# Two column groups of the modulation and the first token block's end, moved into the second feed-forward

## The chip, the cores and the metric

The kernel runs on one core of a Trainium2 chip, in float32. The metric is the device time of one execution in microseconds, in the median of several runs.

## The reference

A transformer block with an mLSTM and one with latent attention, each followed by a PEER layer (top-16 experts out of 16384 for each of 8 heads, gathered by index) and a gated projection, and behind them one modulated block. 256 tokens of width 1024. What the change touches lies in the modulated block:

```python
mod = jax.nn.silu(c) @ w_ada[l] + b_ada[l]
sh1, sc1, g1, sh2, sc2, g2 = jnp.split(mod[:, None, :], 6, axis=-1)
h = modulate(rmsnorm(x, norm_mix_g[l]), sh1, sc1)
x = x + g1 * hybrid_mixer(h, ...)
h = modulate(rmsnorm(x, norm_ffn_g[l]), sh2, sc2)
x = x + g2 * swiglu(h, w_ffn_gate[l], w_ffn_up[l], w_ffn_down[l])
...
return rmsnorm(x, norm_final_g)
```

`w_ada` is 1024 x 6144. `g2`, the last of the six, is its last 1024 columns; it is first used behind the down projection of the feed-forward.

## The kernel before, in words

The 256 tokens are two token blocks (`tb` 0 and 1) of 128. Every engine has its own program, written out by hand; semaphores tie them together. The dense work is cut into slots (generators that all engines step through in the same order). Four windows of expert gathering (two layers by two token blocks) run first, and slots of the token block whose experts are done are woven between the groups of the gathering. All of the modulated block for token block 0, its down projection excepted, is woven into the fourth window. Behind that window stand, with no gathering beside them: the end of the PEER layer and the gated projection for token block 1 (`sum_slots(1, 1)`, `ple_slots(1, 1)`), the mixer for token block 1 (`hybrid_slots(1)`), the mixer's output projection (`out_piece`), the second half of token block 0's down projection (`dnB`), the feed-forward of token block 1 (`ffn_slots(1)`) and its down projection (`dn`).

Weights go through a ring of NW = 4 slots of 128 x 4096 floats. `take` on TensorE records a load in program order and waits for it; SyncE issues the recorded loads in this order, one queue, and load number i first waits until the last reader of load i - 4 is done (L1276). `last_use` or `done` records that reader. `aux` puts other transfers in the same queue. A tile of 1024 x 512 weights is 2048 KB.

The modulation's matrix is used in column groups of 512. Group j through the ring: `ada_load(j)` on TensorE records the load; `ada_part(j)` on VectorE waits for the load and forms the weighted sum over its 8 row chunks in place (one tensor_scalar, L1882, and seven scalar_tensor_tensor, L1884); `ada_sum(j)` on TensorE waits for that and multiplies the sum with a matrix of ones, and it is the last reader of the slot; `ada_gate(j)` on VectorE (L1906) adds the result to the bias in `N["g2"]`. Groups 10 and 11 are `g2`. Before, their four steps stand in `hybrid_slots(1)`: load at the end of slot s, part in s + 2, sum at the start of s + 3, gate in s + 4, with s = 5 for group 10 and s = 9 for group 11.

Slots of `hybrid_slots(1)` around them on TensorE: cmp projection in 2 and 3, `nq` in 4 and 5, `kk` in 6 and 7, the compression matmuls (`compress`, two loads of 1 MB, k and v) in 7, first scores and the compression's gather matmuls (`gather_compressed`) in 9, `vv` (280 columns, 1120 KB) in 10, the second layer of the compression in 11, `bq` in 12 and 13, `bk` in 14 and 15, `bv` in 16 and 17, then four merge gates, two merge projections.

`ffn_slots(tb)` on TensorE: for each of six groups of up to 512 hidden columns (FGROUPS; the sixth has 256) a gate tile `fg` and an up tile `fu`, each one load and 64 matmuls of 128 x 128 (32 in the sixth). ScalarE evacuates `fg` with Silu, VectorE multiplies with `fu` (`product`, L2541). Down group g waits for product g.

The first token block's end on VectorE: behind the two additions of `dnB` (L2592) the multiplication with `g2` (L2594), `gated_add(0)` (L2505) and `final_norm(0)` (sum of squares L2322, a square root on ScalarE, L2583), then the copy to `out` by SyncE behind all loads.

Of the kernel before, what the change touches and what calls it, by code (L numbers as in the profile page):

```python
# [10 lines left out]
ALU = mybir.AluOpType  # L11
# [48 lines left out]
ADA_GATES = (10, 11)  # L60
# [38 lines left out]
NSA_BEFORE = (0, 2 * len(NSA_HEADS[0]))  # L99
SB_BEFORE = (0, len(SB_HEADS[0]))  # L100

ADA_AT = {5: 10, 9: 11}

PLAN = ((FIRST_SLOTS, 5, GROUPS - 4), (NEXT_SLOTS, 0, GROUPS - 2), (NEXT_SLOTS, 0, GROUPS - 2), (LAST_SLOTS, 0, GROUPS - 2))

# [48 lines left out]
def program(nc, a, out, ctx, dbg):  # L154
# [186 lines left out]
    def _(pe):  # L341
# [36 lines left out]
        def last_use(rec, name):  # L378
            b, k = place[name]
            rec["done"] = (bank_full[b], k + 1)  # L380

        def ada_load(j):
            i = nw[0]
            nw[0] += 1
            rec = dict(kind="w", src=rows(a["w_ada_2"][0], j * 512, 512), slot=i % NW, i=i, kc=KC, n=512, p=P, done=None)
            loads.append(rec)
            ada_order.append(j)
            ada_at[j] = (i % NW, 16 * (i // NW + 1), rec)

        def ada_sum(j):  # L390
            slot, _, rec = ada_at[j]
            pe.wait_ge(sem("ada_part"), ada_order.index(j) + 1)
            o = open_(f"ada{j}")
            close(mm(o[:, :], ones[:, :], ring[:, slot, (KC - 1) * 512:KC * 512]), f"ada{j}")
            last_use(rec, f"ada{j}")
# [495 lines left out]
        def ffn_slots(tb):  # L891
            await_T("xT7", tb)
            for g, chs in enumerate(FGROUPS):
                n = len(chs) * P
                for nm, w_dram in ((f"fg{tb}_{g}", a["w_ffn_gate_2"][0]), (f"fu{tb}_{g}", a["w_ffn_up_2"][0])):
                    w, rec = take(rows(w_dram, chs[0] * P, n), KC, n)
                    o = open_(nm)
                    for e in range(len(chs)):
                        ins = feat(o, e * P, w, xT, slice(e * P, (e + 1) * P), range(KC), KC, cols(tb))
                        if e % 2 == 1:  # L900
                            if e == len(chs) - 1:
                                close(ins, nm)
                                last_use(rec, nm)
                            yield f"ffn {nm} {e}"
            yield "ffn last silu"
            yield "ffn last product"
# [33 lines left out]
        def hybrid_slots(tb):  # L940
# [201 lines left out]
                    close(mm(o[:, 0:16], maskQ[:, kv * P:(kv + 1) * P], gatherT[:, :]), nm)  # L1142

            for i in range(plan["n"]):
                if tb == 1:
                    for s, j in ADA_AT.items():
                        if i == s + 3:
                            ada_sum(j)
                for g, s in enumerate(plan["nsa"]):
                    if i == s + 4:  # L1150
                        nT(g)
# [62 lines left out]
                for half in range(2):  # L1214
# [3 lines left out]
                    if i == plan["yb"] + half:  # L1218
                        moved(pe, f"bO_{tb}")
                        merge("yb", a["w_proj_b_2"][0], X["obT"], half)  # L1220
                if tb == 1 and i in ADA_AT:
                    ada_load(ADA_AT[i])
                yield f"hybrid {i}"

        def last_slots():
# [181 lines left out]
    def _(act):  # L1407
# [16 lines left out]
        def sqrt(n):  # L1424
            nsq[0] += 1
            act.wait_ge(sem("var_ready"), nsq[0])
            f(sdv[:, 0:n], var[:, 0:n], ACT.Sqrt).then_inc(sem("sd_ready"), 1)
# [361 lines left out]
        def ffn_slots(tb):  # L1789
            for g, chs in enumerate(FGROUPS):  # L1790
                for x in range(2):
                    for e in range(-(-len(chs) // 2)):
                        if x == 1 and e == 0:
                            evac(f"fg{tb}_{g}", B[tb]["hid"][:, chs[0]:chs[-1] + 1, :], split(len(chs)), fn=ACT.Silu)
                        yield f"ffn {g} {x} {e}"
            yield "ffn last silu"
            yield "ffn last product"
# [18 lines left out]
            pass  # L1816
        sqrt(1)
        evac_norm("xT7", 1, 1)
        sqrt(1)
        for _ in ffn_slots(1):  # L1820
            pass
        sqrt(1)

    @block.vector
    def _(dve):
# [52 lines left out]
        def ada_part(j):  # L1878
            slot, loaded, _ = ada_at[j]
            dve.wait_ge(slot_loaded[slot], loaded)  # L1880
            w = ring[:, slot, :].rearrange("p (k n) -> p k n", k=KC)
            step(v.tensor_scalar(w[:, 0, :], w[:, 0, :], scT[:, 0:1], None, ALU.mult))  # L1882
            for k in range(1, KC):
                ins = v.scalar_tensor_tensor(w[:, k, :], w[:, k, :], scT[:, k:k + 1], w[:, k - 1, :], ALU.mult, ALU.add)  # L1884
                if k < KC - 1:
                    step(ins)
            ins.then_inc(sem("ada_part"), 1)
# [456 lines left out]
        def hybrid_slots(tb):  # L2344
# [63 lines left out]
            for i in range(plan["n"]):  # L2408
# [64 lines left out]
                for half in range(2):  # L2473
                    for x, at in enumerate((plan["ya"], plan["yb"])):
                        if i == at + 1 + half:
# [7 lines left out]
                            if x == 1:  # L2483
                                v.tensor_tensor(X["yT"][:, 4 * half:4 * half + 4, :], sg, X["sg"][2 * half], ALU.add
                                                ).then_inc(sem("yT"), 1)
                if tb == 1:
                    for s, j in ADA_AT.items():
                        if i == s + 2:
                            ada_part(j)
                        if i == s + 4:  # L2490
                            if j in ADA_GATES:
                                ada_gate(j)
                            else:
                                ada_column(j)
                yield f"hybrid {i}"

        def gated_half(name, tb, half, g, scale):
# [89 lines left out]
        for half in range(2):  # L2587
# [3 lines left out]
            ps = full(dve, nm)  # L2591
            free(v.tensor_tensor(yt[:, 0, cs], ps[:, :], yt[:, 0, cs], ALU.add), nm)  # L2592
            moved(dve, nm)
        step(v.tensor_tensor(yt[:, 0, :], yt[:, 0, :], N["g2"], ALU.mult))  # L2594
        gated_add(0)
        final_norm(0)
        for _ in ffn_slots(1):
            pass
        for half in range(2):
            cs = slice(half * 512, half * 512 + 512)  # L2600
            nm = f"dn_{half}"
# [62 lines left out]
```

## Time and profile before

| | |
|---|---|
| median of 3 runs | 2200.2 us |
| the three runs | 2190.97, 2200.2, 3935.1 us |
| profiled execution | 2203.15 us |
| span of its trace | 2201.4 us |
| busy in it: TensorE, VectorE, ScalarE, GpSimd | 1702.9, 1219.4, 925.0, 662.8 us |
| mean bandwidth | 366 GB/s |

The span is that of all engines' instructions in one profiled execution; times in rows count from its start. The expert gathering ends at about 1855 us; what the change touches lies behind it.

### The profile page before, as it was taken

The page shows a single profiled execution, that of the slowest core. Times are in us where ns is not written, and L with a number is a line of the kernel's source. Part 1 is how long each engine was busy: PE and PEld are TensorE (multiplying, and loading weights), DVE is VectorE, ACT ScalarE, POOL GpSimd, SP SyncE. Part 2 cuts the span into 40 slices and gives each one's busy share as a digit, 9 for nine tenths or more (in the row PEclk, how much of TensorE's full clock was granted, in tenths as well). Part 3 has the DMA queues.
Part 4 walks back from the last instruction along what each step waited for, and adds up shares of the span by engine and source line. Part 5 has one row for each costly group of instructions (what it writes and reads, how often), then busy time and mean ns, then how long its engine had stood idle before and what let it go on. Part 6 is the DMA issues. An engine that isn't in the chain of part 4 may idle for free.

```text
span 2201.4 us, 26815 instructions
## 1 busy us (share of the span) xinstructions
PE 1702.9 (77%) x10480; PEld 1404.5 (64%) x10480; DVE 1219.4 (55%) x3088; ACT 925.0 (42%) x1325; POOL 662.8 (30%) x632
## 2 busy tenths in 40 slices
PE   7889766555688778557888875767976887889998
PEld 5447765454567668545766865566875886569694
DVE  5766778787644556975454688555444423252201
ACT  1011545455545543554555455455633533334000
POOL 2841243344433333343334333442222221000000
PEclk9989887678889689778888876888998988989999
DMA  8947999999999999999999999999999997784775
GB/s 319 333 144 286 400 410 416 416 402 420 410 403 415 413 416 378 411 391 404 416 413 417 415 383 384 414 402 407 407 414 406 411 399 296 280 306 165 275 256 202
DMA packets 196718, 806.71 MB, mean 366 GB/s; under 512 B 11984, under 2 KB 21824, under 8 KB 129904
## 3 DMA queue, kind: packets, MB, share of 16 engines
q0 software_dynamic: 76256, 545.07, 60.5%
q1 hardware_dynamic: 119760, 259.27, 31.9%
q8 instruction: 83, 1.36, 0.3%
q10 hardware_dynamic: 576, 0.66, 0.1%
q14 instruction: 43, 0.35, 0.0%
HBM read 803.90 MB, written 1.05 MB: 366 GB/s over the span
## 4 chain that ended last, share of the span: by engine, by line
PE 36%; DMA 34%; DVE 15%; ACT 5%; issue 3%; POOL 3%; SPq 2%; POOLq 0%; DVEq 0%
PE bank L364 28%; DMA arena<-in_uv,eidx 20%; PE bank L619 8%; DVE arena L2110 6%; DMA ring<-in_w_in_2r 5%; DMA ring<-in_peer_w_q 5%; POOL arena L1400 3%; ACT arena L1412 2%; DMA ring<-in_w_out 2%; DMA ring<-in_w_ffn_gate 2%; SPq L1276 2%; DVE y_tok L2041 1%; DVE y_tok L2037 1%; ACT L1412 1%; DVE y_tok L2077 1%
## 5 line engine op out<-in xcount | busy, mean ns | idle before, releaser
L619 PE MATMUL bank<-ident,arena 128*128 128x128 f32 x4096 | 657.1, 326 | 344.1 <-ACT arena L1412 341.5
L1400 POOL DMA_INDIRECT arena<-in_uv,eidx x512 | 564.5, 1103 | 1118.5 <-PE bank L619 974.2
L2110 DVE CUSTOM_DVE_ANT_0 arena<-arena,x_tok 128x1024 f32<-128x1024 f32 x512 | 620.5, 1224 | 418.0 <-DMA arena<-in_uv,eidx 411.5
L619 PEld LDWEIGHTS bank<-ident,arena 128*128 128x128 f32 x4096 | 580.7, 169 | 420.4 <-ACT arena L1412 403.8
L1412 ACT ACTIVATE arena<-arena,coef 128x1024 f32<-128x1024 f32 x512 | 560.0, 1142 | 135.7 <-DVE coef L2121 134.9
L364 PE MATMUL bank<-xT,ring 128*128 128x128 f32 (+2 forms) x3680 | 466.2, 289 | 61.2 <-DMA ring<-in_peer_w_q 22.6
L364 PEld LDWEIGHTS bank<-xT,ring 128*128 128x128 f32 (+1 forms) x3680 | 447.1, 199 | 77.8 <-DMA ring<-in_peer_w_q 22.4
L1412 ACT ACTIVATE glu<-dots 128x2 f32<-128x2 f32 x256 | 52.2, 204 | 538.3 <-DVE dots L2110 522.8
L364 PE MATMUL bank<-ring,xT 128*128 128x512 f32 (+3 forms) x384 | 164.1, 582 | 24.9 <-DMA ring<-in_w_in_2r 19.2
L1412 ACT ACT_TABLE_LOAD x119 | 152.7, 1283 | 2.9 <-PEq L2656 0.8
L364 PEld LDWEIGHTS bank<-ring,xT 128*128 128x128 f32 x384 | 77.2, 207 | 98.0 <-issue 66.8
L364 PE MATMUL bank<-ring,mid_region 128*128 128x512 f32 (+2 forms) x392 | 117.5, 465 | 17.4 <-DMA ring<-in_w_out 15.4
L1412 ACT ACTIVATE arena<-bank 128x512 f32<-128x512 f32 (+2 forms) x57 | 29.5, 541 | 225.4 <-PE bank L364 221.1
L364 PEld LDWEIGHTS bank<-ring,mid_region 128*128 128x128 f32 (+1 forms) x392 | 59.1, 192 | 65.3 <-issue 46.1
L1412 ACT ACTIVATE mid_region<-bank 128x512 f32<-128x512 f32 (+7 forms) x113 | 50.9, 473 | 115.6 <-PE bank L364 115.2
L2121 DVE TENSOR_TENSOR coef<-glu,gate 128x2 f32<-128x2 f32 x256 | 41.2, 161 | 99.8 <-ACT glu L1412 96.0
L364 PE MATMUL bank<-ring,arena 128*128 128x512 f32 (+1 forms) x248 | 84.0, 519 | 4.4 <-DMA ring<-in_cmp_w_v 1.8
L364 PEld LDWEIGHTS bank<-ring,arena 128*128 128x128 f32 (+1 forms) x248 | 36.8, 172 | 47.9 <-issue 45.7
L364 PE MATMUL bank<-mid_region 128*128 128x128 f32 (+8 forms) x280 | 54.5, 348 | 2.8 <-ACT mid_region L1412 2.8
L1884 DVE SCALAR_TENSOR_TENSOR ring<-ring,silu_cT 128x512 f32<-128x512 f32 x63 | 52.5, 833 | 2.2
L364 PEld LDWEIGHTS bank<-mid_region 128*128 128x128 f32 (+4 forms) x280 | 41.0, 209 | 13.8 <-issue 8.3
L1412 ACT ACTIVATE sdv<-var 128x1 f32<-128x1 f32 (+2 forms) x17 | 3.5, 204 | 109.9 <-DVE var L2324 78.5
(266 smaller groups left out, 1203.8 us busy)
## 6 DMA issues: line engine op xcount, KB each, us to landing
ring<-in_w_in_2r SPq DMA_DIRECT2D x20, 2048.0 KB
ring<-in_peer_w_q SPq DMA_DIRECT2D x16, 2048.0 KB
ring<-in_w_ffn_gate SPq DMA_DIRECT2D x10, 2048.0 KB
ring<-in_w_ffn_up SPq DMA_DIRECT2D x10, 2048.0 KB
ring<-in_w_ffn_down SPq DMA_DIRECT2D x10, 2048.0 KB
ring<-in_w_ada SPq DMA_DIRECT2D x9, 2048.0 KB
ring<-in_ple_w_gate SPq DMA_DIRECT2D x8, 2048.0 KB
ring<-in_a_w_in SPq DMA_DIRECT2D x6, 2048.0 KB
```

The source lines that it names most:

```text
L364: return nc.tensor.matmul(o, l, r, start=start, stop=stop)
L619: ins = nc.tensor.matmul(bank(f"pe{l}_{tb}_{c // 4}")[:, (c % 4) * P:(c % 4 + 1) * P], gath[:, s, D + c * P:D + (c + 1) * P], ident[:, :], ...
L1276: sp.dma_start(dst, r["src"]).then_inc(slot_loaded[r["slot"]], 16)
L1400: pool.indirect_dma_start(gath[:, i % SLOTS, :], None, a["uv"], bass.IndirectOffsetOnAxis(ap=eidx[:, tb, i:i + 1], axis=0)).then_inc(sem(f ...
L1412: return nc.scalar.activation(o, i, fn, **kw)
L1884: ins = v.scalar_tensor_tensor(w[:, k, :], w[:, k, :], scT[:, k:k + 1], w[:, k - 1, :], ALU.mult, ALU.add)
L2037: step.go(v.max(vals[:, i, lo:lo + 8], s[:, i, :]))
L2041: step.go(v.max_index(idx[:, i, lo:lo + 8], vals[:, i, lo:lo + 8], s[:, i, :]))
L2077: step(v.tensor_tensor(eq, eq, i4[:, :, e, :].unsqueeze(2).broadcast_to([P, UH, 16, 16]), ALU.mult))
L2110: v.tensor_tensor_reduce(out=gath[:, s, 0:D], in0=gath[:, s, 0:D], in1=xt[:, tb, :], scale=1.0, scalar=0.0, op0=ALU.mult, op1=ALU.add, acc ...
L2121: v.tensor_tensor(coef[:, s:s + GRP], glu[:, s:s + GRP], gate[:, tb, k * GRP:(k + 1) * GRP], ALU.mult).then_inc(sem("coef"), 1)
```

## The change

Column groups 10 and 11 go from the mixer of token block 1 to its feed-forward: load behind the gate tile of groups 0 and 2, part on VectorE in the slot behind that, sum on TensorE behind the gate tile of groups 1 and 3, gate addition on VectorE ahead of groups 2 and 4. Since `g2` is now finished later, the first token block's end, which multiplies with it, moves to the start of the sixth group, with its square root on ScalarE.

```diff
-ADA_AT = {5: 10, 9: 11}
+ADA_AT = {0: 10, 2: 11}
@@ TensorE, ffn_slots
                             if e == len(chs) - 1:
                                 close(ins, nm)
                                 last_use(rec, nm)
+                                if tb == 1 and nm[1] == "g" and g in ADA_AT:
+                                    ada_load(ADA_AT[g])
+                                if tb == 1 and nm[1] == "g" and g - 1 in ADA_AT:
+                                    ada_sum(ADA_AT[g - 1])
                             yield f"ffn {nm} {e}"
@@ TensorE, hybrid_slots
-                if tb == 1:
-                    for s, j in ADA_AT.items():
-                        if i == s + 3:
-                            ada_sum(j)
...
-                if tb == 1 and i in ADA_AT:
-                    ada_load(ADA_AT[i])
@@ ScalarE
         evac_norm("xT7", 1, 1)
-        sqrt(1)
-        for _ in ffn_slots(1):
-            pass
+        for nm in ffn_slots(1):
+            if nm == "ffn 5 0 0":
+                sqrt(1)
         sqrt(1)
@@ VectorE, hybrid_slots
-                if tb == 1:
-                    for s, j in ADA_AT.items():
-                        if i == s + 2:
-                            ada_part(j)
-                        if i == s + 4:
-                            if j in ADA_GATES:
-                                ada_gate(j)
-                            else:
-                                ada_column(j)
@@ VectorE, behind dnB
-        step(v.tensor_tensor(yt[:, 0, :], yt[:, 0, :], N["g2"], ALU.mult))
-        gated_add(0)
-        final_norm(0)
-        for _ in ffn_slots(1):
-            pass
+        for nm in ffn_slots(1):
+            for g, j in ADA_AT.items():
+                if nm == f"ffn {g} 0 1":
+                    ada_part(j)
+                if nm == f"ffn {g + 2} 0 0":
+                    ada_gate(j)
+            if nm == "ffn 5 0 0":
+                step(v.tensor_tensor(yt[:, 0, :], yt[:, 0, :], N["g2"], ALU.mult))
+                gated_add(0)
+                final_norm(0)
```

## Rows read from the trace of the kernel before

**Rows 1.** Windows: busy us of each engine, then granted clock, DMA share, GB/s

```profile
1900.00:1950.00 50.00, 38.38 (x333) 32.75 (x332) 24.11 (x53) 13.21 (x36) 0.00 (x0) 0.89 0.82 284
...
2100.00:2150.00 50.00, 50.00 (x450) 50.00 (x450) 2.75 (x4) 1.79 (x3) 0.00 (x0) 1.00 0.72 252
```

**Rows 2.** Chain that ended last, 1913 to 1933: start us, us, what

```profile
1913.18 6.25 DMA ring<-in_cmp_w_v
...
1921.64 0.37 SPq L1276
...
1922.07 10.97 DMA ring<-in_w_in_2r
```

**Rows 3.** Timeline of TensorE in the mixer: start, us, instructions, idle before

```profile
1902.22 14.45 PE L364 MATMUL bank<-xT,ring 128*128 128x128 f32 x128
...
1919.47 1.08 PE L364 MATMUL bank<-ring,arena 128*32 128x128 f32 x32 [1.79 <-DMA ring<-in_cmp_w_v]
1920.49 1.12 PE L364 MATMUL bank<-ring,ones 128*128 128x512 f32 x2
1921.54 0.49 PE L364 MATMUL bank<-mid_region,arena 64*128 64x128 f32 x4
...
1922.63 0.62 PE L364 MATMUL bank<-gatherT,maskQ 128*128 128x16 f32 x4
1933.08 6.54 PE L364 MATMUL bank<-ring,xT 128*128 128x280 f32 x16 [9.83 <-DMA ring<-in_w_in_2r]
```

**Rows 4.** Timeline of SyncE's queue, the loads ahead

```profile
1890.78 0.37 SPq L1276 DMA_DIRECT2D ring<-in_w_ada  x1
1902.41 0.37 SPq L1276 DMA_DIRECT2D ring<-in_w_in_2r  x1
1906.03 0.71 SPq L1276 DMA_DIRECT2D ring<-in_cmp_w_k  x1
```

**Rows 5.** Timeline of VectorE: partial sums of groups 10 and 11

```profile
1909.48 5.48 DVE L1884 SCALAR_TENSOR_TENSOR ring<-ring,silu_cT 128x512 f32<-128x512 f32 x7
...
1929.91 0.49 DVE L1882 TENSOR_SCALAR ring<-ring,silu_cT 128x512 f32<-128x512 f32 x1 [3.85 <-DMA ring<-in_w_ada]
```

**Rows 6.** Windows, columns as in rows 1, for clock and transfers

```profile
1929.00:1938.00 9.00, 4.92 (x11) 3.62 (x12) 5.75 (x8) 0.00 (x0) 0.00 (x0) 0.50 1.07 379
...
1875.00:1898.00 23.00, 21.03 (x55) 9.50 (x54) 4.91 (x8) 4.34 (x9) 0.00 (x0) 0.98 1.04 396
...
2090.00:2091.00 1.00, 1.00 (x11) 1.00 (x10) 0.00 (x0) 0.00 (x0) 0.00 (x0) 1.00 0.86 303
2091.00:2092.00 1.00, 1.00 (x11) 1.00 (x10) 0.69 (x1) 0.00 (x0) 0.00 (x0) 1.00 0.00 0
...
1922.00:1943.00 21.00, 11.17 (x65) 8.50 (x62) 11.94 (x26) 4.73 (x15) 0.00 (x0) 0.76 1.00 355
```

**Rows 7.** Timelines of TensorE and SyncE behind 1997

```profile
1997.44 0.76 PE L364 MATMUL bank<-arena,upper 128*128 128x128 f32 x2 [3.78 <-ACT arena L1412]
...
2000.13 5.12 PE L364 MATMUL bank<-xT,ring 128*128 128x128 f32 x32
...
2041.80 13.97 PE L364 MATMUL bank<-ring,arena 128*128 128x512 f32 x32 [1.62 <-issue]
...
2076.41 78.85 PE L364 MATMUL bank<-xT,ring 128*128 128x128 f32 x704 [2.61 <-issue]
...
2083.83 0.37 SPq L1276 DMA_DIRECT2D ring<-in_w_ffn_gate  x1
```

**Rows 8.** Timelines of VectorE and ScalarE, 2073 to 2153

```profile
2073.80 1.23 DVE L2594 TENSOR_TENSOR y_tok<-y_tok,mid_region 128x1024 f32<-128x1024 f32 x1
...
2078.21 1.28 DVE L2583 SCALAR_TENSOR_TENSOR y_tok<-x_tok,rstd,lnp 128x1024 f32<-128x1024 f32 x1
...
2148.22 0.69 DVE L2541 TENSOR_TENSOR arena<-arena,bank 128x512 f32<-128x512 f32 x1 [13.61 <-PE bank L364]
...
2152.13 1.28 ACT L1412 ACT_TABLE_LOAD   x1
```

## The prediction

> **What bounds the kernel now.** I read the busy time by stretch first [rows 1]. The kernel up to 1855 us is the gathering of expert rows; the change touches nothing there. In the stretch 1900 to 1950 TensorE is busy 38.38 of 50 us and no other engine is over half; in 2100 to 2150, the second block's feed-forward for token block 1, TensorE is busy all 50 us, VectorE 2.75 us and the DMA engines 0.72 of the time. So behind the gather the end is set by TensorE, and its idle time is what can be won. Then the chain that ended last [rows 2]: it leaves TensorE twice for transfers, once for the second compression weight (issued 1913.18, 6.25 us) and once for the 280 columns of `vv` (issued 1922.07, 10.97 us). Between them stands the queue of SyncE, L1276, at 1921.64. Why the queue issued so late is read from the order of the takes. Load n waits for the release of load n - 4, and the queue issues in order. At 1921.64 it issued column group 11 [rows 2], which waited for the slot of group 10. That slot came free with group 10's ones-matmul at 1920.49 [rows 3]. The `vv` load needs the slot of `kk`, free since about 1916.6, when `compress` could start behind the 128 matmuls begun at 1902.22 [rows 3]. It stood behind group 11 in the queue for nothing of its own, and its data behind group 11's 2.1 MB. TensorE idled 9.83 us before `vv` and 1.79 us before the second compression weight [rows 3].
>
> **The change in the mixer.** All times are those of the trace of before; the new ones are moved on that clock.
>
> Loads: without group 10, `kk` takes the issue of 1890.78, the first compression weight that of 1902.41, the second that of 1906.03 [rows 4], `vv` that of 1913.18 [rows 2]. The compression weight took 6.25 us from issue [rows 2], so it lands at 1912.3, and TensorE asks for it at about 1917.7: the 1.79 us go. TensorE then comes to `vv` where it now ends the gather matmuls, 1922.63 + 0.62 = 1923.2 [rows 3], less 1.79 and less group 10's sum, 1.05 us from its start to the next start: 1920.3. A larger load, 2.1 MB issued alone at 2083.83 [rows 7], kept the DMA engines at work until 2091 and not after [rows 6], 7.2 us; `vv` has 1.15 MB, so 1920.4 is the latest, and 9.6 to 9.8 us go. I take 9.8. The next load, `bq`, then goes out at about 1916.7 and lands, at the 355 to 396 GB/s of [rows 6], at about 1924 to 1925, when TensorE has just done `vv` and the next score matmuls: no wait, or one below 1 us.
>
> Clock: during the idle time the granted clock fell to 0.50, which is the level of 1.2 GHz, and it stayed there for 1929 to 1938 [rows 6]. So `vv` took 6.54 us for 16 matmuls [rows 3]. At full clock, 0.437 us for 512 columns (13.97 us over 32 matmuls, [rows 7]) gives 0.24 us for 280, 3.8 us and about 0.1 for the tail: 2.6 us go. The bound below is 0, if the clock falls for another reason.
>
> Group 11's sum goes too, two matmuls of 512 columns at the 0.437 us of above: 0.9 us. VectorE's weighted sums (0.5 + 5.48 us each, [rows 5]) lay in its idle time. The 7 accumulating steps of group 11 even waited for data. Their going gives nothing, as VectorE waits on TensorE's scores there. Sum of the mixer: 1.8 + 1.05 + 9.8 + 2.6 + 0.9 = 16.2 us, lower bound 13.4.
>
> **What the feed-forward pays.** It is 704 matmuls in 78.85 us [rows 7], 0.112 us each. A tile of 64 takes 7.15 us and uses one load of 2.1 MB. TensorE starts it at 2076.41, so `fg0`, `fu0`, `fg1` end at 2083.6, 2090.8, 2097.9. Two sums are put in, 0.9 us each: 1.8 us. VectorE can make group 10's partial sum in 6 us directly behind the first block's end (2073.8), as that block's last steps no longer stand there.
>
> The new loads take ring slots, so four tiles ahead becomes three. The order is fg0, ada10, fu0, fg1, fu1, fg2, ada11, fu2, fg3, fu3, fg4. Now fg2 waits for group 10's sum, about 2099, where it was issued at 2083.83 [rows 7], and ada11 and fu2, whose slots are free by then, go out right behind. fg2 is wanted at 2106.1. The one row of a first load with others right behind it is group 11 itself: issued 1921.64 [rows 2], taken up by VectorE at 1929.91 [rows 5], 8.3 us. So fg2 lands at 2107.3. fu2 is the third of three, 6.3 MB. Group 11, `vv`, `bq` and `bk` were 7.4 MB and filled 1922 to 1943 at 355 GB/s [rows 6]; of the 21.3 us from the first issue to the end of it, 6.3/7.4 is 18.1: fu2 lands that much behind fg2's issue, at 2117.1. TensorE without waits would want it at 2113.3. The two waits together are 3.8 us. In the same way fg4 waits for group 11's sum behind fg3, and has fu3's 7.15 us to land in 8.3: 1.1 us. fu4 and fg5 follow within the time that fg4 and fu4 take. Cost: 1.8 + 3.8 + 1.1 = 6.7 us. Bounds: at the 396 GB/s of the stretch 1875 to 1898 [rows 6] fu2 lands 16.2 us behind (18.1 x 355/396), waits of 1.9 us, and fg4, landing in 7.2, waits for nothing; loads that don't overlap at all, three times 7.2 us, give 7.4 and 1.1.
>
> Here the row of group 11 stands against a rule. The Trainium skill, DMA: Bandwidth & Descriptors, section Queues, rings and completion order, says that each DMA engine consumes the descriptors of one ring in order. By that, fg2 would not suffer from the loads behind it and would land in 7.2 us with no wait, and fg4 too, and the sum would be smaller by 1.1 us, as fu2, behind all bytes, lands when it did.
>
> Clock here: a wait of 3.78 us before 1997.44 was followed by 32 matmuls in 5.12 us [rows 7] where 32 at 0.112 and the tail make 3.8, and the small ones ahead of them lost about as much: 2.5 us in all. The 2.6 us of idle before 2076.41 were followed by 0.112 us a matmul, full clock. The waits I expect are 1.2, 2.6 and 1.1 us, nearest to the second row: I charge nothing and keep 2.5 for the bound.
>
> **The first block's end.** VectorE's gating, addition and final norm of token block 0 ran from 2073.80 to 2079.49 [rows 8], 5.7 us. TensorE meanwhile waited for ScalarE's `xT`, which doesn't depend on them, and VectorE has little else to do in the feed-forward, 2.75 us in 50 [rows 1]. Gain of the removal: 0. In the new place they start behind the product of 2148.22 to 2148.91 and last 5.7 us, and ScalarE must change tables for the square root and back, 1.28 us each [rows 8]. The variance is there 4.0 us into the chain (5.7 less the last step's 1.28 and 0.4 for root and reciprocal), then 0.2 for the root, 1.28 for the table and, estimated from its 256 columns, 0.4 for the last silu: 5.9 us behind 2148.9, where the last product is wanted 7.15 us behind 2148.2. It fits by 0.5 us. Should it not, `down` asks for that product only at its sixth group, about 30 us later. SyncE's copy of that half of the result stands behind the last down load at 2169 in any case. Cost 0.
>
> **Sum.** -16.2 + 6.7 = -9.5 us. The profiled execution took 2203.15 us (span 2201.4), so 2193.6; the median of the runs shown is 2200.2, 3 us lower, so 2190.7, and I say 2191. By the bounds the likeliest case runs from -12.5 (-16.2 + 1.8 + 1.9) to -0.6 (-13.4 + 10.3 + 2.5).
>
> **Rivals.**
> 1. The feed-forward hides its new loads (its DMA share is 0.72, [rows 1]): only the two sums are paid, net -14.4, 2186. Against it: bytes behind one another from 2099 on can't land three in 14.2 us at the rate of [rows 6]. Chance 0.15.
> 2. The wait moves inside the mixer: with `vv` early, TensorE waits for `bq`, issued close behind, or for the compression's ScalarE chain, and the clock falls all the same. Half of the 9.8 and all of the 2.6 are not won: net -2, 2198. For it: `bq` fits by a microsecond at most. Chance 0.15.
> 3. Slower: the clock falls at each of the three new waits of the feed-forward and stays down as long as in [rows 6], some 10 us, 5 us lost each on dense matmuls. 15 + 6.7 against 16.2 is +5.5, 2206. It decides from 9.5 us of loss, 19 us at half clock. For it: the wait of 3.78 us was followed by low clock [rows 7]; against it: TensorE at work got its clock back 5 us after 1933. Chance 0.08.
> 4. The first block's end is late and delays the last product past down's sixth group: needs 30 us; chance below 0.02.
>
> The forecast has 0.6. The range must also take the runs' own spread, 2190.97 to 2203.15 for one kernel: 2180 to 2204, from rival 1 less 6 to rival 2 plus 6; the likeliest alone 2187 to 2200. What this kernel's measurement can tell from no change is about 2%, 44 us: no case reaches it. Faster by more 0.02, within 0.97, slower by more 0.01.
>
> **What would show it.** Right: no idle of TensorE before `vv` and a granted clock of 1.0 over it; `vv` load issued with the end of `nq`; hybrid about 16 us shorter; in the feed-forward waits for `in_w_ffn_gate` or `in_w_ffn_up` at the third group (two, together about 4 us) and one at the fifth (about 1); the last product at its old distance from fu5. Wrong: a wait of several us for `in_w_in_2r` at `bq`; a low clock behind the feed-forward's waits; waits of TensorE for VectorE before a group's sum.

## The result, and the profile after

The changed kernel takes 2189.2 us in the median of 12 runs, the kernel before 2197.8 us in its 12. One of these 12, of 3935.1 us, is left out of the ratio. The ratio is 0.9966, 95% interval 0.9956 to 0.9976: 7.5 us less, interval 5.3 to 9.7 (the two medians are 8.6 us apart). In what follows, a gain against the kernel before is worked out from such a ratio unless medians are named.

The profiled execution took 2192.36 us (span 2190.6) against 2203.15 (2201.4). The two spans differ by 10.8 us, more than the times do. 4.6 us of that lie ahead of the mixer, where the two kernels do the same, and 1.7 us are the 8 matmuls of the first line below, whose clock turns out to differ between executions of one kernel.

The mixer first. This is the timeline of TensorE in the changed kernel, the stretch of [rows 3]; start us, us, instructions, and in brackets the idle time before:

```profile
1892.46 3.60 PE L364 MATMUL bank<-ring,mid_region 128*128 128x512 f32 x8
1895.90 14.45 PE L364 MATMUL bank<-xT,ring 128*128 128x128 f32 x128
1910.28 1.96 PE L364 MATMUL bank<-ring,arena 128*32 128x128 f32 x64
...
1913.26 0.62 PE L364 MATMUL bank<-gatherT,maskQ 128*128 128x16 f32 x4
1913.72 4.02 PE L364 MATMUL bank<-ring,xT 128*128 128x280 f32 x16
...
1920.37 3.84 PE L364 MATMUL bank<-xT,ring 128*128 128x128 f32 x32 [0.95 <-DMA ring<-in_w_in_2r]
...
2019.02 13.97 PE L364 MATMUL bank<-ring,arena 128*128 128x512 f32 x32 [1.62 <-issue]
```

The two compression weights run in one piece of 64 matmuls, and `vv` starts 17.8 us behind the 128 matmuls, where it started 30.9 us behind them in [rows 3]: it comes 13.0 us earlier. It takes 4.02 us instead of 6.54. A window over it (busy us of PE, PEld, DVE, ACT, POOL, then granted clock, DMA share, GB/s) has the full clock, where [rows 6] have 0.50:

```profile
1913.00:1918.00 5.00, 5.00 (x30) 3.87 (x30) 3.11 (x8) 3.89 (x9) 0.00 (x0) 1.00 1.04 393
```

A wait of 0.95 us has come before the next load, `bq`.

The feed-forward of token block 1, TensorE in the changed kernel; in [rows 7] this was one piece of 704 matmuls:

```profile
2053.64 23.30 PE L364 MATMUL bank<-xT,ring 128*128 128x128 f32 x192 [2.61 <-issue]
2076.78 1.02 PE L364 MATMUL bank<-ring,ones 128*128 128x512 f32 x2
2077.64 7.31 PE L364 MATMUL bank<-xT,ring 128*128 128x128 f32 x64
2085.66 7.41 PE L364 MATMUL bank<-xT,ring 128*128 128x128 f32 x64 [0.71 <-DMA ring<-in_w_ffn_gate]
2097.84 16.18 PE L364 MATMUL bank<-xT,ring 128*128 128x128 f32 x128 [4.77 <-DMA ring<-in_w_ffn_up]
2113.86 1.02 PE L364 MATMUL bank<-ring,ones 128*128 128x512 f32 x2
2114.72 7.31 PE L364 MATMUL bank<-xT,ring 128*128 128x128 f32 x64
2122.80 21.70 PE L364 MATMUL bank<-xT,ring 128*128 128x128 f32 x192 [0.77 <-DMA ring<-in_w_ffn_gate]
2144.34 37.93 PE L364 MATMUL bank<-ring,arena 128*128 128x512 f32 x88
```

It now takes 90.7 us to the first down matmul, where it took 78.7. One reads off three waits, before fg2 (the gate tile of group 2), fu2 (its up tile) and fg4, of 0.71, 4.77 and 0.77 us, and the two ones-matmuls. The queue of SyncE shows where the longest comes from:

```profile
2062.68 0.37 SPq L1274 DMA_DIRECT2D ring<-in_w_ffn_up  x1
2077.84 0.37 SPq L1274 DMA_DIRECT2D ring<-in_w_ffn_gate  x1
2078.25 0.58 SPq L1274 DMA_DIRECT2D ring<-in_w_ada  x1
2078.88 3.05 SPq L1274 DMA_DIRECT2D ring<-in_w_ffn_up  x1
2084.98 3.08 SPq L1274 DMA_DIRECT2D ring<-in_w_ffn_gate  x1
```

Between fu1's issue and fg2's the queue issues nothing for 15 us; then the issues of three loads start within 1.0 us, as soon as group 10's sum is done. VectorE had finished its part of group 10 long before. The second of the three loads, group 11, is taken up by VectorE 14.6 us behind the first issue:

```profile
2051.55 5.48 DVE L1882 SCALAR_TENSOR_TENSOR ring<-ring,silu_cT 128x512 f32<-128x512 f32 x7
...
2092.47 0.49 DVE L1880 TENSOR_SCALAR ring<-ring,silu_cT 128x512 f32<-128x512 f32 x1 [5.82 <-DMA ring<-in_w_ada]
```

So group 10 lay ready in its slot from 2057.0 until its ones-matmul at 2076.78, 19.7 us: the slot was held by the place of that matmul in TensorE's program, and by nothing that it waited for. The load behind the longest wait, fu2's, stands as one piece in the chain that ended last:

```profile
2078.88 18.92 DMA ring<-in_w_ffn_up
```

The parts, as three stretches of each trace. "Mixer" runs from the start of the 128 matmuls to that of the output projection (2019.02 above), "feed-forward" from its first matmul to the first down matmul; the 34.6 us between them are the same in all of them (in "sum in idle time" one ones-matmul lies there too). All three are in us. The 8 matmuls are those of the first line above, behind a wait of 1.97 us. The last four rows are one profiled run each, to be read for their traces; a single run says nothing of a few us. Each ratio is against runs of the kernel before that were taken beside the version (their medians are 2195.3 to 2197.8 us), so ratios, and not medians, are compared across rows.

| kernel | 8 matmuls | mixer | feed-forward | median us | ratio to before (interval) |
|---|---|---|---|---|---|
| before | 5.30 | 139.6 | 78.7 | 2197.8 | |
| change | 3.60 | 123.1 | 90.7 | 2189.2 | 0.9966 (0.9956 to 0.9976) |
| no groups | 3.60 | 122.8 | 80.3 | 2180.7 | 0.9917 (0.9904 to 0.9931) |
| end only | 5.30 | 139.5 | 78.7 | 2194.6 | 0.9990 (0.9977 to 1.0002) |
| early sums | 3.60 | 122.4 | 82.0 | 2184.0 | 0.9933 (0.9921 to 0.9944) |
| early sum of 10 | 3.60 | 121.6 | 81.2 | 2183.6 | 0.9939 (0.9925 to 0.9952) |
| only 10 moved | 3.60 | 132.1 | 80.7 | 2190.2 | 0.9971 (0.9960 to 0.9982) |
| 10 early in the mixer | 3.60 | 132.8 | 80.3 | 2191.0 | 0.9973 (0.9959 to 0.9987) |
| sum in idle time | 3.60 | 123.0 | 79.5 | 2177.8 | 0.9914 (0.9901 to 0.9927) |
| 11 third in line | 3.60 | 122.9 | 86.2 | 2187.5 | 0.9963 (0.9947 to 0.9979) |
| change again | 3.60 | 124.5 | 88.6 | 2188.5, one run | |
| before again | 5.23 | 139.3 | 78.7 | 2200.3, one run | |
| before, third time | 3.60 | 136.6 | 80.3 | 2193.1, one run | |
| 10 early in the mixer, again | 5.30 | 136.3 | 78.7 | 2196.1, one run | |

### The profile page after: what moved, and what is told of

Its sections match the earlier page's. It is cut to its first block, busy times and chain, and to the rows that moved or that the text cites. A ratio compares the mean times of both kernels' runs of the same rounds, so it can differ in the third digit from the quotient of the medians.

```text
span 2190.6 us, 26817 instructions
## 1 busy us (share of the span) xinstructions
PE 1692.5 (77%) x10480; PEld 1399.7 (64%) x10480; DVE 1216.9 (56%) x3088; ACT 926.1 (42%) x1327; POOL 668.1 (30%) x632
## 3 DMA queue, kind: packets, MB, share of 16 engines
HBM read 803.90 MB, written 1.05 MB: 367 GB/s over the span
## 4 chain that ended last, share of the span: by engine, by line
DMA 37%; PE 35%; DVE 15%; ACT 4%; issue 3%; POOL 3%; SPq 0%; POOLq 0%; DVEq 0%
PE bank L364 26%; DMA arena<-in_uv,eidx 20%; PE bank L619 8%; DVE arena L2108 6%; DMA ring<-in_w_in_2r 5%; DMA ring<-in_w_ffn_up 5%; DMA ring<-in_peer_w_q 4%; POOL arena L1398 3%; ACT arena L1410 2%; DMA ring<-in_w_out 2%; DVE y_tok L2039 1%; DVE y_tok L2035 1%; DVE y_tok L2075 1%; DVE y_tok L2076 1%; ACT L1410 1%
## 5 line engine op out<-in xcount | busy, mean ns | idle before, releaser
L1398 POOL DMA_INDIRECT arena<-in_uv,eidx x512 | 572.7, 1119 | 1111.0 <-PE bank L619 967.2
L364 PE MATMUL bank<-mid_region 128*128 128x128 f32 (+8 forms) x280 | 49.0, 327 | 2.7 <-ACT mid_region L1410 2.7
L364 PE MATMUL bank<-mid_region,ring 128*128 128x128 f32 x336 | 42.2, 289 | 7.2 <-ACT mid_region L1410 7.2
```

The source lines that it names most:

```text
L364: return nc.tensor.matmul(o, l, r, start=start, stop=stop)
L1398: pool.indirect_dma_start(gath[:, i % SLOTS, :], None, a["uv"], bass.IndirectOffsetOnAxis(ap=eidx[:, tb, i:i + 1], axis=0)).then_inc(sem(f ...
```

## The experiments

**No groups.** The change with both groups left out, so that `g2` is its bias alone and the kernel doesn't compute the whole block; everything else stands.

```diff
-ADA_AT = {0: 10, 2: 11}
+ADA_AT = {}
```

> The changed kernel with column groups 10 and 11 left out altogether: no load, partial sum, ones-matmul or gate addition, so g2 is its bias alone. Theory (slot order): the change wins the waits and the low clock around vv in the mixer and pays in the feed-forward for late loads. Then this kernel keeps the mixer's gain, 15 to 17 us, and has a feed-forward of 79 us for token block 1 with no wait for a load: 15 to 17 us faster than before (ratio 0.992 to 0.993), 8 to 9 us faster than the change. Rival (the change's gain is small because the mixer's gain was small, and the feed-forward costs next to nothing): this kernel is at most 2 us faster than the change.

Measured: 0.9917, 18 us faster than before (interval 15 to 21), where 15 to 17 was expected. Against the change it is 8.5 us faster by the medians and 10.8 by the two ratios, where 8 to 9 was expected. Feed-forward:

```profile
2054.25 80.48 PE L364 MATMUL bank<-xT,ring 128*128 128x128 f32 x704 [2.61 <-issue]
```

One piece again, without a wait for a load. So the small gain of the change is a large one in the mixer less what the feed-forward gives back; the rival (at most 2 us faster than the change) falls.

**End only.** The kernel before with the first token block's end at the start of the sixth group, and on ScalarE its square root (not shown) in the same place.

```diff
-        step(v.tensor_tensor(yt[:, 0, :], yt[:, 0, :], N["g2"], ALU.mult))
-        gated_add(0)
-        final_norm(0)
-        for _ in ffn_slots(1):
-            pass
+        for nm in ffn_slots(1):
+            if nm == "ffn 5 0 0":
+                step(v.tensor_tensor(yt[:, 0, :], yt[:, 0, :], N["g2"], ALU.mult))
+                gated_add(0)
+                final_norm(0)
...
```

> The kernel before with only the first token block's end moved to the start of the sixth group of the feed-forward; groups 10 and 11 stay in the mixer. Theory: 0 us, ratio 1.000 within 0.001; the last product comes at its old distance, 7.15 us behind the product before it. Rival (the end stood in the way of the feed-forward's start, or delays its last product and with it the down projection): a gain or loss of 1 to 6 us, seen as another idle time of TensorE before the feed-forward or before its last down group.

Measured: 0.9990, interval 0.9977 to 1.0002: 2.2 us faster at the middle, and no change lies inside. Timelines of TensorE and VectorE:

```profile
2067.88 78.85 PE L364 MATMUL bank<-xT,ring 128*128 128x128 f32 x704 [2.60 <-issue]
...
2139.69 0.69 DVE L2541 TENSOR_TENSOR arena<-arena,bank 128x512 f32<-128x512 f32 x1 [13.61 <-PE bank L364]
...
2144.94 1.28 DVE L2583 SCALAR_TENSOR_TENSOR y_tok<-x_tok,rstd,lnp 128x1024 f32<-128x1024 f32 x1
2146.84 0.42 DVE L2541 TENSOR_TENSOR arena<-arena,bank 128x256 f32<-128x256 f32 x1 [0.62 <-PE bank L364]
```

The feed-forward has its 78.85 us and its wait of 2.60 us ahead, to 0.01 us those of [rows 7]. The end is over 0.62 us before the last product, which comes 7.15 us behind the one before it. No stretch of the trace shows a gain, so by the trace this part is worth nothing; the times alone don't exclude 2 us.

**Early sums.** Both ones-matmuls one tile earlier.

```diff
-                                if tb == 1 and nm[1] == "g" and g - 1 in ADA_AT:
-                                    ada_sum(ADA_AT[g - 1])
+                                if tb == 1 and nm[1] == "u" and g in ADA_AT:
+                                    ada_sum(ADA_AT[g])
```

> The change with both ones-matmuls one tile earlier: group 10's behind the up tile of group 0, group 11's behind the up tile of group 2. Theory (slot order): fg2 is issued 7 us earlier, so the waits for fg2, fu2 and fg4 (0.7, 4.8, 0.8 us) go, and the low clock behind fu2's wait with them; the feed-forward takes 81 to 83 us instead of 90.7; 6 to 8 us faster than the change, ratio to before 0.993 to 0.994. Rival (bytes: 4.2 MB more in the same stretch cost their transfer time wherever the sums stand): the waits move to other tiles and the feed-forward keeps 88 us or more; no more than 2 us faster than the change.

Measured: 0.9933; against the change 5.2 us faster by the medians and 7.3 by the ratios (6 to 8 expected). Timeline of TensorE:

```profile
2054.01 16.16 PE L364 MATMUL bank<-xT,ring 128*128 128x128 f32 x128 [2.60 <-issue]
2070.01 1.02 PE L364 MATMUL bank<-ring,ones 128*128 128x512 f32 x2
2070.87 28.75 PE L364 MATMUL bank<-xT,ring 128*128 128x128 f32 x256
2099.45 1.02 PE L364 MATMUL bank<-ring,ones 128*128 128x512 f32 x2
2100.31 35.89 PE L364 MATMUL bank<-xT,ring 128*128 128x128 f32 x320
2136.04 37.93 PE L364 MATMUL bank<-ring,arena 128*128 128x512 f32 x88
```

The same instructions and the same bytes, and none of the three waits is left. The feed-forward's 82.0 us are the 78.7 of before, 1.7 for the two sums and 1.6 of low clock at its start (128 matmuls in 16.16 us, where the next version has 14.53). What the feed-forward of the change paid beyond the sums came from when a slot was given back, and not from the 4.2 MB more that it carried.

**Early sum of group 10 alone.** Group 11's stays behind the gate tile of group 3.

```diff
-                                if tb == 1 and nm[1] == "g" and g - 1 in ADA_AT:
-                                    ada_sum(ADA_AT[g - 1])
+                                if tb == 1 and (nm[1], g) in (("u", 0), ("g", 3)):
+                                    ada_sum(ADA_AT[0 if g == 0 else 2])
```

> The change with group 10's ones-matmul alone one tile earlier (behind the up tile of group 0); group 11's stays behind the gate tile of group 3. Theory (slot order): the waits for fg2 and fu2 go, that for fg4 (0.8 us) stays; feed-forward 82 to 84 us. Rival (bytes): as in the run with both, waits move on and nothing is won.

Measured: 0.9939, feed-forward 81.2 us (expected 82 to 84; the clock was full from its start here). One wait is left, and it is the one named:

```profile
2113.13 21.70 PE L364 MATMUL bank<-xT,ring 128*128 128x128 f32 x192 [0.56 <-DMA ring<-in_w_ffn_gate]
```

So the waits for fg2 and fu2 belong to group 10's sum, that for fg4 to group 11's.

**Only group 10 moved.** Group 11 has its four steps in the mixer as before (the lines that put them there, by `MIX_AT`, aren't shown).

```diff
-ADA_AT = {0: 10, 2: 11}
+ADA_AT = {0: 10}
+MIX_AT = {9: 11}
...
```

> The change with group 11 put back into the mixer (load behind slot 9 as before); group 10 and the first block's end stay in the feed-forward. Theory (slot order): group 11's load now waits for the release of nq's slot, 1913.2 on the clock of the kernel before, and vv's load for kk's, 1916.7; vv then lands at about 1924.6 and TensorE asks for it at 1920.3: a wait of 3.5 to 5 us instead of 9.8 (0 in the change). In the feed-forward the wait for fg2 stays (0.7 to 1.3), the one for fu2 is below 1 and the one for fg4 is gone. Mixer gain 9 to 11, feed-forward cost 2 to 4: 6 to 8 us faster than before, about as the change. Rival (bytes): half of the traffic moved gives half of each, a wait of about 5 us at vv and of about 2.4 at fu2.

Measured: 0.9971, about as the change. TensorE, at `vv` and at fg2:

```profile
1913.96 6.60 PE L365 MATMUL bank<-ring,xT 128*128 128x280 f32 x16 [5.33 <-DMA ring<-in_w_in_2r]
...
2087.96 50.29 PE L365 MATMUL bank<-xT,ring 128*128 128x128 f32 x448 [0.87 <-DMA ring<-in_w_ffn_gate]
```

The wait before `vv` is a little above the 3.5 to 5 us expected; fu2 and fg4 wait for nothing, and the feed-forward costs 2.0 us more than before. The rival's 2.4 us at fu2 are not there, so it falls, though its 5 us at `vv` came. `vv` ran at low clock behind 5.33 us of idle too (6.60 us, where the change has 4.02).

**Group 10 earlier within the mixer.** The kernel before; VectorE's part in slot 4 and the ones-matmul in slot 6, nothing in the feed-forward.

```diff
-                        if i == s + 3:
+                        if i == (6 if j == 10 else s + 3):
                             ada_sum(j)
...
-                        if i == s + 2:
+                        if i == (4 if j == 10 else s + 2):
                             ada_part(j)
```

> The kernel before, nothing moved to the feed-forward, with group 10's partial sum on VectorE in slot 4 of the mixer instead of 7 and its ones-matmul in slot 6 instead of 8. Theory (slot order): the slot of group 10 comes free 7 us earlier (about 1914 on the clock of before), group 11 goes out at 1914.3, vv at 1917.7, and the wait before vv falls from 9.8 us to 2 to 4 us; the one before the second compression weight stays; 6 to 9 us faster than before with the same bytes in the same stage. Rival (bytes): the 4.2 MB are what costs, the wait stays above 8 us and the time within 2 us of before.

Measured: 0.9973, 5.9 us faster than before (interval 3 to 9), with 6 to 9 expected. The time fits the theory at its lower end; the wait doesn't. It fell to 6.82 us (7.24 in the second trace), not to 2 to 4:

```profile
1923.27 6.09 PE L364 MATMUL bank<-ring,xT 128*128 128x280 f32 x16 [6.82 <-DMA ring<-in_w_in_2r]
...
1907.05 0.70 SPq L1276 DMA_DIRECT2D ring<-in_cmp_w_v  x1
1907.85 2.41 SPq L1276 DMA_DIRECT2D ring<-in_w_ada  x1
1911.42 5.06 SPq L1276 DMA_DIRECT2D ring<-in_w_in_2r  x2
```

(The last line holds the issues of `vv` and `bq`.) Counted from the start of the 128 matmuls, `vv` is issued some 4.5 us earlier than in the kernel before, as expected. But it landed 11.9 us behind its issue: three loads of 4.3 MB now stand in a row and take 16.2 us from the first issue. They didn't quite have the transfers to themselves. From 1907 to 1908 the DMA engines moved 33 GB/s, so nearly nothing was left of earlier loads, and from 1908 until `vv` landed they moved 5.1 MB, 0.8 more than the three loads hold. Other queues moved 0.02 MB, so the 0.8 MB are of loads queued behind the three. So the rival as stated (a wait above 8 us, within 2 us of before) falls, but what it named is there in part: the earlier slot brings the issue forward, and the traffic takes part of that back.

Counted from the 128 matmuls, `vv` starts 27.2 and 27.3 us behind them in the two traces of this kernel, and 30.2 to 30.9 us in the three of before. These 3 to 4 us are what the traces show surely; the rest of the 5.9 us lies in places whose clock differs between executions.

For a learner this run matters as much as the change itself: it moves nothing to another stage, puts one reader earlier, and its ratio (0.9973, interval 0.9959 to 0.9987) can't be told from the change's 0.9966.

**Group 11 third in line.** The change with group 11's load behind fu2's.

```diff
-                                if tb == 1 and nm[1] == "g" and g in ADA_AT:
+                                if tb == 1 and (nm[1], g) in (("g", 0), ("u", 2)):
                                     ada_load(ADA_AT[g])
```

> The change with only the load of group 11 moved, from behind the gate tile of group 2 to behind its up tile, so that fu2 stands second in the queue behind fg2 and group 11 third; both ones-matmuls as in the change. Theory (slot order and place in the queue): the wait for fg2 (0.7 us) stays, as group 10's sum is still late; the wait for fu2 falls from 4.8 us to 0 to 0.7, as it is the second and not the third transfer behind fg2's issue; that for fg4 goes, as its load now follows fu2's slot. Feed-forward 81 to 83.5 us instead of 90.7, 5 to 8 us faster than the change. Rival (the late sum is the cause by itself, the place in the queue is not): the wait for fu2 stays above 3 us and no more than 2 us are won.

Measured: 0.9963, the same as the change within the intervals; the 5 to 8 us expected are missed. The feed-forward takes 86.2 us, and not 81 to 83.5. fu2's and fg4's waits are gone as expected, but one that I had not expected has come, for fg3:

```profile
2084.78 14.56 PE L364 MATMUL bank<-xT,ring 128*128 128x128 f32 x128 [0.70 <-DMA ring<-in_w_ffn_gate]
2102.29 7.41 PE L364 MATMUL bank<-xT,ring 128*128 128x128 f32 x64 [2.96 <-DMA ring<-in_w_ffn_gate]
```

Four loads land from the issue at 2076.97 to 2102.29, 25.3 us, where three took 20.0 in the change. The late sum leaves a backlog of one load more than there is time for; whoever stands behind group 11 pays. The trace wins 2.4 us in the feed-forward against the second trace of the change, or 4 with equal clock at its start; the times show less than that, 0.7 us by the ratios. Of the versions run here, only those with an earlier sum are without the backlog.

**Sum in idle time.** Early sums, and group 10 ahead of the feed-forward: its load during token block 0's down projection, its ones-matmul in the wait of 2.6 us.

```diff
-ADA_AT = {0: 10, 2: 11}
+ADA_AT = {2: 11}
...
+                if (g, half) == (DOWN_FIRST + 1, 0):
+                    ada_load(10)
         transposes("xT7", yt, KC, 1, xn_ready[1], 2)
+        ada_sum(10)
...
             pass
+        ada_part(10)
...
         for nm in ffn_slots(1):
+            if nm == "ffn 1 0 0":
+                ada_gate(10)
```

The lines not shown are those of early sums.

> The version with both sums early, and group 10 moved further ahead: its load behind the second weight of token block 0's down projection, its partial sum on VectorE in the 11 us in which it waits for that projection, its ones-matmul in the 2.6 us in which TensorE waits for ScalarE ahead of the feed-forward; group 11 as in the version with early sums. Theory (slot order, work in idle time costs nothing): 0.9 us less for the sum and no new wait, feed-forward 80 to 81.5 us, 1 to 2.5 us faster than the version with early sums. Rival (one slot less ahead of the feed-forward's first tiles makes fu0 or fg1 late): a wait of 1 to 4 us there, no faster than the version with early sums.

Measured: 0.9914, 18.9 us faster than before, 11 faster than the change, and level with the kernel that leaves the groups out (0.9917). TensorE:

```profile
2048.72 1.02 PE L364 MATMUL bank<-ring,ones 128*128 128x512 f32 x2
2051.49 43.12 PE L364 MATMUL bank<-xT,ring 128*128 128x128 f32 x384 [1.74 <-issue]
```

The wait has shrunk from 2.6 to 1.74 us, and the ones-matmul fills the rest; the feed-forward takes 79.5 us, 0.9 more than before for the one sum left in it. It is the fastest complete kernel of the study. Neither fu0 nor fg1 waits, so the rival falls. Against the version with early sums it is 4 us faster by the two ratios, whose intervals overlap. In the feed-forwards of the two traces 2.5 us are seen, 0.9 for the sum and 1.6 of clock, the next point; the rest is not explained.

**The same kernels again.** Unchanged copies, to look at the clock behind waits that all kernels have.

> The changed kernel once more, to see its granted clock behind two waits that every run so far has alike, 1.97 us ahead of the mixer and 2.61 us ahead of the feed-forward. Theory: whether the clock falls behind them differs from execution to execution, 1.7 us each, and belongs to no kernel; so one of the two may now be otherwise than in the first trace (full behind the first, low behind the second). Waits for fg2, fu2 and fg4 as before within 0.5 us. Rival: the low clock behind the second belongs to the change and comes again in the same place.

> The kernel before once more, for the same question. Its first trace had low clock behind the 1.97 us ahead of the mixer and full clock behind the 2.61 us ahead of the feed-forward. Theory: this may differ now; the wait before vv is 9.0 to 10.0 us again with low clock over vv, as a wait of that length always had it. Rival: both places as in the first trace.

> The kernel before a third time. In both earlier traces of it, and in that of the kernel with the end alone moved, the 8 matmuls behind the 1.97 us wait ahead of the mixer took 5.2 to 5.3 us (low clock), in all nine traces of other kernels 3.6 us. Theory (differs from execution to execution): 3.6 us may be seen here. Rival (it belongs to the kernel before, so the change wins 1.7 us there): 5.2 to 5.3 us again. Low clock over vv behind a wait of 9 to 10 us in either case.

> The kernel before with group 10's partial sum and ones-matmul early in the mixer, once more. Up to that place it issues the instructions of the kernel before, and its first trace had 3.6 us for the 8 matmuls. Theory (differs from execution to execution): 5.2 us may be seen. Rival (belongs to the kernel): 3.6 us again. The wait before vv 6 to 7.5 us again.

The first of these is the change: its feed-forward started at full clock this time, 192 matmuls in 21.68 us against 23.30 above, with the same 2.61 us of idle ahead:

```profile
2051.80 21.68 PE L364 MATMUL bank<-xT,ring 128*128 128x128 f32 x192 [2.61 <-issue]
...
2094.06 16.19 PE L364 MATMUL bank<-xT,ring 128*128 128x128 f32 x128 [4.42 <-DMA ring<-in_w_ffn_up]
```

The second trace of the kernel before was like its first. The third was not, in either place:

```profile
1890.15 3.60 PE L364 MATMUL bank<-ring,mid_region 128*128 128x512 f32 x8
...
2064.79 80.48 PE L364 MATMUL bank<-xT,ring 128*128 128x128 f32 x704 [2.60 <-issue]
```

And the kernel with group 10 early in the mixer had 5.30 us in its second trace for the 8 matmuls, after 3.60 in its first. Both levels follow the same wait in the same kernel: the 1.6 to 1.7 us belong to the execution. The rivals of the first, third and fourth copy, which tie them to a kernel, fall; that of the second, both places as in its first trace, came. For comparing two traces that means: where one has low clock behind such a wait and the other has not, take 1.7 us off before a stretch is read.

## Why the prediction was right, point by point

I forecast 2191 us, 9.5 us less than before; measured are 2189 and 7.5 us less, with interval 5.3 to 9.7, no change beyond 2%. That the time itself came out within 2 us is in part luck: the gain was forecast 2 us too large, and the three runs that I counted from had a median of 2200.2 us, where all 12 have 2197.8.

*The mixer, 16.2 us expected.* Waits and group 10's sum: `vv` starts 13.0 us earlier, 12.7 expected (1.8 + 1.05 + 9.8). The clock over `vv`: 2.5 us, 2.6 expected. Group 11's sum: 0.9 us, as expected, but a wait of 0.95 us before `bq` comes in, the "below 1 us" that I had named and priced at nothing. So at `bq` the gain is 15.4 us. To the end of the mixer it is 16.5 in the first traces, as the low clock behind the wait of 3.78 us lasted less long (32 matmuls in 3.92 us, not the 5.12 of [rows 7]), and 12.1 to 16.5 between the three traces of before and the two of the change, whose clocks differ. Kernels without the groups in the mixer had 121.6 to 124.5 us, those of before 136.6 to 139.6. One row was misread on the way, without weight in the sum: of group 11 it is the scaling step that waited 3.85 us for data [rows 5], and not the 7 accumulating ones.

*The feed-forward, 6.7 us expected, 9.9 and 12.0 in the two traces.* The mechanism was right to the tile: fg2, fu2, fg4, in that order of cause. Terms: the sums 1.7 (1.8 expected); the waits for fg2 and fu2 together 5.5 and 5.2 us where 3.8 was expected (fg2 0.7 and 0.8 for 1.2, fu2 4.8 and 4.4 for 2.6); fg4 0.8 and 0.6 where 1.1 was. The mis-sized step is the 18.1 us for fu2 as third of three loads, which came from a stretch average of [rows 6]: it took 20.0 (2077.84 to 2097.84) and 19.7. The single load fg2 took 7.8, between the 7.2 of a load alone and the 8.3 of group 11. The other one is the clock, which I charged at nothing because I expected a wait of 2.6 us there: behind fu2's wait of 4.4 to 4.8 us 128 matmuls took 16.2 us instead of 14.5 in both traces, 1.7 us. A window right behind it (columns as in the window above) shows it:

```profile
2098.00:2101.00 3.00, 3.00 (x17) 3.00 (x18) 0.47 (x1) 0.00 (x0) 0.00 (x0) 0.57 1.05 386
```

That makes 9.7 and 9.2 us. Up to the measured ones, 0.7 us in either trace are what breaking the row of matmuls costs by itself: a piece of 64 takes 7.31 or 7.41 us, where one inside a long row takes 7.15. The last 1.6 us of the 12.0 are the low clock at the start of the first trace, which belongs to the execution.

*In-order rings.* The Trainium skill, DMA: Bandwidth & Descriptors, section Queues, rings and completion order, has descriptors of one ring consumed in order, by which fg2 would have landed as if alone, in 7.2 us. It took 7.8 and 7.9 with two loads of 2.1 MB right behind it: between the 7.2 and the 8.3 us I took, a little nearer to the latter. The two figures don't measure quite the same, as 7.2 us is until the DMA engines stood still and 7.8 until TensorE went on. A view of the transfers from fg2's issue until TensorE takes it (2077.84 to 2085.66) shows 0.3 MB more than the 2.1 MB of that load (no transfer ran just before it, 0 GB/s from 2076.5 to 2077.84):

```profile
DMA packets 1188, 2.40 MB, mean 307 GB/s; under 512 B 16, under 2 KB 16, under 8 KB 1188
```

So part of the loads behind had moved before the first was taken up, 0.8 us of transfers at the 386 GB/s of the window above. Each DMA engine can still have kept its order; the views don't part the engines. The order of landing was that of issue wherever a wait shows it.

*The first token block's end, 0 us.* Right: the root and the tables fitted, with about the room that was worked out. The last silu ended at 2144.20, 0.4 us ahead of the last product:

```profile
2137.49 0.69 DVE L2530 TENSOR_TENSOR arena<-arena,bank 128x512 f32<-128x512 f32 x1 [13.76 <-PE bank L364]
...
2142.74 1.28 DVE L2572 SCALAR_TENSOR_TENSOR y_tok<-x_tok,rstd,lnp 128x1024 f32<-128x1024 f32 x1
2143.82 0.38 ACT L1410 ACTIVATE arena<-bank 128x256 f32<-128x256 f32 x1
...
2144.61 0.42 DVE L2530 TENSOR_TENSOR arena<-arena,bank 128x256 f32<-128x256 f32 x1 [0.59 <-PE bank L364]
```

*The rivals.* Hidden loads (rival 1) were not seen in the change, but the version with early sums is that case, at 2184.0 us where the rival had 2186, and it needed one tile's difference in place. A wait moved inside the mixer (rival 2) came, with 0.95 of the 4.9 us it was given, and the clock did not fall. The clock (rival 3) fell behind one of the three new waits, the longest, and cost 1.7 us, not 5. The last product was not late (rival 4).

*The sum.* Terms in the traces: -15.4 and +9.9 are -5.5 us, plus what the clocks of the execution add on either side; the times say -7.5, interval 5.3 to 9.7. The forecast's -9.5 lies at the edge of that interval: the mixer was right within a microsecond, and the feed-forward was under-priced by 3.2 us in one trace and 5.3 in the other, 1.6 of which are the clock at its start.

What stays open: the 2 us by which the times of "end only" and of the change lie below what the stretches of their traces show. The gathering ahead ends between 1845 and 1856 us in the traces that I read there, without an order that I could tie to an edit.

## What to carry to other kernels

In a ring of slots with one queue, a load's cost is where its slot is given back: count, for each load, which reader frees the slot n places on, and put that reader as early as its data allow, or into time in which its engine waits anyway. Moving work to a stage with idle transfer time (0.72 busy) won 7.5 us; giving the slots back one tile earlier there won 5 to 7 more, and with the reader in a wait of 2.6 us the kernel was as fast as one without the work. Try the place of the reader first: within the old stage alone it won 5.9 us. Ask also how long a slot is held for nothing, as here for 19.7 us between the end of VectorE's part and the ones-matmul. And a removed wait can count more than its length: the 9.8 us of wait before `vv` were followed by low clock, which took 2.5 us more over the matmuls behind it.

## What the runs showed of the hardware

- The same wait of TensorE is followed by either clock, in different executions of one kernel: behind 1.97 us, 8 matmuls of 512 columns in 3.60 or 5.2 to 5.3 us (low in 4 of 14 traces); behind 2.6 us, 704 matmuls in 78.85 or 80.48. In the mixer and the feed-forward of token block 1, waits of 4.4, 5.3 and longer were followed by low clock in every trace. One of 2.96 us ("11 third in line") was followed by full clock, 64 matmuls in 7.41 us. Behind the wait of 3.8 us [rows 7] the first matmuls were slow in every trace, but for different lengths: the 32 that follow 2.7 us later took 3.80 to 5.38 us.
- Three loads of 2.1 MB whose issues start within 1 us on one queue were taken up 7.8, 14.6 and 20.0 us behind the first issue; a fourth, issued 7.1 us behind the first, at 25.3. A row of small and large ones (1.05, 2.1, 1.15 MB) took 16.2 us for 4.3 MB, more than the 12.1 that the average rate of a busy stretch (355 GB/s, [rows 6]) gives. In both cases more bytes moved by then than these loads hold: 2.40 MB instead of 2.10 when the first was taken up, and 5.1 instead of 4.3.
